# The up projection of a feed-forward block: the norm's root applied to the finished tiles in PSUM instead of to its input

## The reference

```python
y = memory_cross_attention(h, ...)          # ends in o @ wo, MEM_INNER 512 -> 2048
x = x + rmsnorm(y, g[3])
h = rmsnorm(x, g[4])
y = conv_ffn(h, ffn_w_up, ffn_conv_w, ffn_conv_b, ffn_w_down)

def rmsnorm(x, gain):
    return x * rsqrt(mean(x * x, axis=-1) + 1e-6) * gain

def conv_ffn(h, w_up, conv_w, conv_b, w_down):
    up = h @ w_up                           # [256, 11264]
    up_pad = pad(up, 2 tokens in front)
    conv = conv_b + sum(up_pad[:, j:j + s] * conv_w[j] for j in range(3))
    gate, val = split(conv, 2)
    return (gelu(gate) * val) @ w_down
```

## Time and profile before

| what | us |
|---|---|
| median of 3 runs (3180.01 to 3181.32) | 3180.11 |
| the profiled execution | 3179.2 |
| its span | 3177.4 |
| TensorE busy | 3040.5 |
| VectorE busy | 1570.8 |
| ScalarE busy | 1266.5 |

### The profile page before, as it was taken

One profiled execution on the slowest core, in us unless ns is written; L12 is line 12 of the kernel. 1 busy time (PEld: TensorE's weight loads), 2 busy tenths in 40 slices (PEclk: granted clock), 3 DMA queues, 4 the chain that ended last, 5 costly groups with the idle time before them and its releaser, 6 DMA issues.

```text
span 3177.4 us, 51930 instructions
## 1 busy us (share of the span) xinstructions
PE 3040.5 (96%) x21496; PEld 2642.4 (83%) x21496; DVE 1570.8 (49%) x2402; ACT 1266.5 (40%) x1925; POOL 17.9 (1%) x34
## 2 busy tenths in 40 slices
PE   6999999899889999999998999999999999999997
PEld 6966666698779999999996888778878998889896
DVE  4444434544365556564445323554553474247744
ACT  4322112343445444443434223444542472245544
POOL 0000000000000000000000000000000000000000
PEclk9999999899989999999999999999999999999998
DMA  7577777544435555545553222222223443234442
GB/s 231 183 292 313 311 316 286 199 141 151 146 119 183 179 181 184 182 156 181 175 191 110 93 93 80 80 80 90 91 99 119 159 161 105 92 118 146 141 152 106
DMA packets 74279, 509.69 MB, mean 160 GB/s; under 512 B 8460, under 2 KB 8588, under 8 KB 20240
## 3 DMA queue, kind: packets, MB, share of 16 engines
q1 hardware_dynamic: 70416, 486.08, 42.9%
q0 software_dynamic: 3712, 21.40, 2.1%
HBM read 500.89 MB, written 6.55 MB: 160 GB/s over the span
## 4 chain that ended last, share of the span: by engine, by line
PE 87%; DVE 6%; ACT 3%; DMA 2%; issue 1%; SPq 0%; ACTq 0%; DVEq 0%
PE bank L685 39%; PE bank L1220 8%; PE bank L780 5%; PE bank L1251 5%; PE bank L1253 5%; PE bank L1252 5%; PE bank L797 2%; PE bank L730 1%; PE bank L731 1%; PE bank L732 1%; PE bank L936 1%; PE bank L876 1%; DMA high_f<-in_w_in 1%; DVE ring_f32r L1972 1%; PE bank L1289 1%
## 5 line engine op out<-in xcount | busy, mean ns | idle before, releaser
L1972 DVE TENSOR_TENSOR ring_f32r<-ring_f,high_f32r 128x1024 fp32r<-128x1024 f32 (+1 forms) x692 | 780.7, 1159 | 794.8 <-ACT high_f32r L1405 793.5
L1405 ACT CAST high_f32r<-ring_f 128x1024 fp32r<-128x1024 f32 (+1 forms) x692 | 655.8, 997 | 881.4 <-PE bank L685 535.9
L685 PE MATMUL bank<-y_f32r,high_f32r 128*128 128x256 f32 (+1 forms) x2784 | 852.6, 306 | 23.3 <-DVE ring_f32r L1972 10.9
L685 PE MATMUL bank<-h_f32r,high_f32r 128*128 128x256 f32 (+1 forms) x2208 | 685.9, 311 | 4.3 <-DVE y_f32r L1972 3.4
L685 PE MATMUL bank<-y_f32r,ring_f32r 128*128 128x256 f32 (+1 forms) x2208 | 673.3, 305 | 0.0
L685 PEld LDWEIGHTS bank<-y_f32r,high_f32r 128*128 128x128 f32 x2784 | 535.3, 192 | 47.1 <-issue 22.2
L685 PEld LDWEIGHTS bank<-h_f32r,high_f32r 128*128 128x128 f32 x2208 | 422.9, 192 | 26.7 <-issue 4.5
L685 PEld LDWEIGHTS bank<-y_f32r,ring_f32r 128*128 128x128 f32 x2208 | 424.2, 192 | 17.2
L1251 PE MATMUL bank<-h_f32r,high_f32r 128*128 128x512 f32 x512 | 209.3, 409 | 0.0
L780 PE MATMUL bank<-h_f,high_f 128*128 128x256 f32 x768 | 196.4, 394 | 9.5 <-DMA high_f<-in_w_in 9.5
L1253 PE MATMUL bank<-h_f32r,ring_f32r 128*128 128x512 f32 x512 | 200.1, 391 | 0.0
(11 more groups left out here) (413 smaller groups left out, 4925.1 us busy)
## 6 DMA issues: line engine op xcount, KB each, us to landing
ring_f<-in_w_in SPq DMA_DIRECT2D x135, 1024.0 KB, 4.9
ring_f<-in_w_mod SPq DMA_DIRECT2D x96, 1024.0 KB, 8.9
ring_f<-in_w_up SPq DMA_DIRECT2D x88, 1024.0 KB, 4.9
ring_f<-in_w_out SPq DMA_DIRECT2D x56, 1024.0 KB, 4.9
ring_f<-in_w_down SPq DMA_DIRECT2D x64, 704.0 KB, 4.0
high_f<-in_w_in SPq DMA_DIRECT2D x24, 1024.0 KB, 5.0
ring_f<-in_w_kv SPq DMA_DIRECT2D x8, 1024.0 KB, 5.0
ring_f<-in_w_q SPq DMA_DIRECT2D x4, 1024.0 KB, 4.9
```

The lines of the kernel that those rows point to most:

```text
L685: last = mm(bk[(t0 + j) % banks][:, 0:width], w[:, c], x[:, k], start=(k == 0 and w is hi and x is rhs.hi), stop=(k == KC - 1 and w is lo))
L1405: act.copy(w_hi[p % 2][:, half], slot[s % SLOTS][:, half]).then_inc(w_high, 1)
L1972: return v.tensor_tensor(out, in0, in1, op)
```

## The change

- ACT's copy of each `wo` tile to Z takes the gain of the first norm with it as a scale column.
- DVE multiplies Z by the root alone, in pieces of 1024 columns, and adds it to x; between the quarters it makes the low halves of H.
- H is now x times the gain of the second norm, without the root. ACT makes it, four instructions of 256 columns per quarter, and casts the quarter right behind it.
- ACT squares x afterwards, into 16 free tiles of Z. PE sums these squares between up tiles 1 and 2, and the second root is made from there.
- DVE multiplies every finished up tile by the root, in its bank, before ACT reads it. ACT waits for that (`f_scaled`) instead of for the tile.

```diff
+        up_sq = Z[:, 16:32]
...
             finish_sum(T, 7)
-            colsum4(H[0], T, 7)
-            gemm3("up")
+            gemm3("up", 0, 2)
+            colsum4(up_sq, T, 7)
+            gemm3("up", 2, 86, rhs="up")
...
                 b = bk[(TILE0["wo"] + n) % 2][:, 0:T]
-                act.copy(Z[:, n, :], b)
+                f(Z[:, n, :], b, ACT.Identity, scale=vec("g")[:, 3 * KC + n:3 * KC + n + 1])
...
             root()
-            squares_of_x(2)
+            for q in range(4):
+                act.wait_ge(x_ready, 4 + q + 1)
+                for k in range(4 * q, 4 * q + 4):
+                    last = f(H[0][:, k, :], X[0][:, k, :], ACT.Identity, scale=vec("g")[:, 4 * KC + k:4 * KC + k + 1])
+                last.then_inc(rhs_made, 1)
+                rhs_highs("up", (q,))
+            for q in range(4):
+                f(up_sq[:, 4 * q:4 * q + 4], X[0][:, 4 * q:4 * q + 4], ACT.Square).then_inc(sq_ready, 1)
             root()
-
-            rhs_highs("up")
...
-                act.wait_ge(gemm_done, i * 4 + (TILE0["up"] + j + 1))
+                act.wait_ge(S("f_scaled"), i * 4 + (j + 1))
...
             rstd(D, RMS1_EPS, parts=True)
             for q in range(4):
-                add_quarter(Z[:, 0:16], gains(3), q)
+                c = slice(4 * q, 4 * q + 4)
+                step(tt(Z[:, c], Z[:, c], spread(stat[:, 0:T], 4)))
+                tt(X[0][:, c], X[0][:, c], Z[:, c], ALU.add).then_inc(x_ready, 1)
+                if q:
+                    rhs_low("up", q - 1)
+            rhs_low("up", 3)
             rstd(D, RMS1_EPS, parts=True)
-            rhs_made_and_split("up", norm_quarter(H[0], X[0], gains(4)))
...
             def up(j, i, ahead=("up", 2)):
+                par, b, c = at(convf, i * 4 + j), bk[(TILE0["up"] + j) % 4], cv[j % 4]
+                dve.wait_ge(gemm_done, i * 4 + (TILE0["up"] + j + 1))
+                tt(b[:, 0:T], b[:, 0:T], stat[:, 0:T]).then_inc(S("f_scaled"), 1)
                 dve.wait_ge(S("f_part"), i * 4 + (j + 1))
-                par, b, c = at(convf, i * 4 + j), bk[(TILE0["up"] + j) % 4], cv[j % 4]
```

## The result

| | before | changed |
|---|---|---|
| median of 20 runs, us | 3179.41 | 3186.76 |
| lowest to highest | 3176.32 to 3183.39 | 3183.87 to 3191.16 |
| the profiled execution | 3179.2 | 3191.16 |
| its span | 3177.4 | 3189.2 |

The changed kernel takes 1.0023 times as long, with an interval of 1.0017 to 1.0028: 7.4 us more, by the interval 5.4 to 8.9. The forecast of 3185.4 is 1.4 us under the median, and its range held it. The kernel is slower clear of the noise; the 6.4 us that I called no change lie inside the interval, so on which side of them it falls is not settled. The difference itself was forecast at 5.3 us, just under the interval.

What follows compares the result with a forecast made beforehand. PE, busy 3040.5 of 3177.4 us, was taken as the bound. Terms -2.0 + 1.6 + 2.1 + 1.9 + 1.7 = +5.3 us on 3179.2 give 3184.5, plus 0.9 for the median: 3185.4 us, range 3180.5 to 3190.

Steps and rivals of the forecast that it cites:

- steps 1 to 7: Chain from the first norm through tiles 0, 1 and the sum: tile 2 starts at 905.95, 2.0 us earlier.
- step 3: ACT makes H, casts it, DVE subtracts: PE starts tile 0 at 877.45, 16 us earlier than now.
- step 8: Half clock returns in tile 2 after the hole, the first one hidden by tile 0's quarters: 1.6 us lost.
- step 5: Sum of squares behind tile 1: PE's small matmuls take 2.4 us, end at 897.0, and the root is there at 901.1.
- The mark: Start of tile 2 in the kernel before, taken as about 907.98, against which the new start was compared.
- half of either is lost: Half clock after the hole, held 2.7 or 3.8 us: a loss of 1.35 to 1.9 us, taken as 1.6.
- The loop: Up tiles: 88 scalings of 0.42 us, 37 us of DVE work, leave 0.95 us of room, so 86 tiles cost nothing.
- The second rival: Scaling in the bank dearer than a read: at 1.6 us each the kernel takes 3203 us; chance 0.05.
- The two places behind DVE's splits: After tiles 62 and 86 ACT waits for a scaling behind DVE's split: PE's waits grow by 2.1 and 1.9 us.
- I count one fall: +1.7: PE's clock falls behind only one of the two late waits of about 3.0 and 2.9 us, costing 1.7 us.
- shifts with it and grows no further: PE's 2.69 us wait, following the one after tile 86's split, moves later without getting longer.
- The first rival: Clock falls in both late stalls behind DVE's splits: 1.7 us more, +7.0 in all, 3187.1 us; chance 0.33.

Runs made afterwards that it cites:

- e3: Changed kernel with the scalings of tiles 63 and 87 put between the halves of DVE's split of finished tiles: 3183.29 us, 1.0013 of before.
- e2: Changed kernel without the scaling in the bank (second root made, not applied), so the new front alone: 3178.91 us, 0.9998 of before.
- e10: Second run of the changed kernel without the scaling in the bank: 3178.39 us, 0.9998 of before.
- e1: Kernel before with only the scaling of each up tile in its bank added (root applied twice): 3184.08 us, 1.0012 of before.
- e9: Second run of the kernel before with only the scaling in the bank added: 3183.33 us, 1.0011 of before.
- the fastest version: Changed kernel, sum between tiles 0 and 1, tile 2's weights before tile 0's scaling, late scalings between split halves: 3171.80 us (0.9980), again 3172.31 (0.9981).
- e5: Changed kernel with the weight halves of tiles 2 and 3 made ahead of the second root: 3177.77 us, 0.9999 of before.
- e6: Changed kernel, weights of tiles 2 and 3 ahead of the second root, late scalings between DVE's split halves: 3173.74 us, 0.9985 of before.

## Why the prediction was right, and where not

**The path to tile 2 (steps 1 to 7): right in kind, 1.2 us off.** Seen from the norm's sum, tile 2 starts after 41.26 us, where the steps give 40.03 (865.92 to 905.95). Tile 0's first matmul at 880.85 is the 877.45 of step 3 moved by 3.4, and the last low half at 889.49 is its 886.1; up to there the steps hold. Tile 0's last quarter then ran mostly at half clock (until 892.7), which step 8 had as hidden, and the sum ended about 0.5 us later than in step 5. ACT's root came as expected, but DVE's reciprocal began 0.95 us after its last instruction for 0.60 before, with ACT's 0.42 in between. Between the end of the reciprocal and the scaling, and between the scaling and ACT, lie 0.3 and 0.27 us where I had put 0.05 in all: the chain shows DVE's sequencer at L2379 there, the entry of the loop over the tiles. Before, that entry lay beside tile 0.

The mark was misread as well. 907.98 is about when tile 1 is handed to ACT; tile 2's first matmul is at 907.59, and 905.95 was compared with the wrong one. Both together turn the forecast of 2.0 us earlier into 0.4.

**Step 8: right that the half clock comes back, too small.** I took 1.6 us. It lasted 5.9 us of work, and from tile 2's start to the first late wait's end it is 4.75 us more than before, of which the wait is 2.09: the half clock cost 2.66. In the five traces with this hole it lasted 2.9, 3.3, 5.8, 5.9 and 6.2 us. The step's "half of either is lost" is a little too much: at half clock 26 matmuls were busy in 5.60 us, at full clock 47 in 5.70 (e3), so 0.44 of the time is lost. Its 2.7 and 3.8 us were the lengths of the stretches asked for; the clock came back after 2.9 and 4.1. The front, forecast at 0.4 us faster, was 2.25 slower in this execution (2.66 less 0.41), and level by the ratios of e2 and e10, where the half clock was short.

**The loop: right.** 88 scalings at 432 ns are 38 us of DVE and move no ordinary tile. The second rival had nothing: the room was 0.95 us and the excess over a read 0.01.

**The two places behind DVE's splits: right to 0.1 us.** Forecast +2.1 and +1.9; the waits grew from 0.89 to 2.98 and from 1.01 to 2.82. e1 and e9 show them without the new front, e2 and e10 the front without them, and e3 that the order of two instructions makes 2.3 us of it.

**The clock behind them is the step that failed: "I count one fall: +1.7".** In this execution it fell behind both. The first fall lasted for 5.9 us of work: from the first late wait's end to the second's it is 142.07 us for 137.69, 4.38 more, of which the second wait's growth is 1.81 and the fall 2.57. The second fall lasted 3.4 us and cost nothing, since the third wait ends 6.9 us behind the second whatever the clock does in between, and shrank from 2.69 to 1.20. That give-back was in none of my steps; I had written that this wait "shifts with it and grows no further", which was true and missed that it can shrink. In all five traces with a fall behind the second wait, the way from that wait's end to the second model is the 268.18 us of before, to 0.01.

The sum by measured distances is -0.41 + 2.66 + 2.09 + 1.81 + 2.57 + 0 = 8.72, and the trace has 8.7. Against the 5.3 forecast the front's path gave 1.6 less, step 8 cost 1.1 more and the late clock 0.9 more, all to the same side. That the forecast time is still only 1.4 us off is partly luck: the 3 runs that I started from had a median 0.7 above that of the 20, and the medians differ by 7.4, less than the 8.7 of the profiled executions.

The first rival, both falls and 3187.1, named what happened in this execution, and of the cases it came nearest to the median. But its price was wrong: it gave the second fall 1.7 us, which was worth nothing, and took the first for 1.7 where it cost 2.6. The Trainium skill's page "TensorE: Matmul & The Clock Gate", in its section "HAM oscillation — how this bites in real kernels", warns of long idle gaps between bursts of matmuls; that its rule covers waits as short as these was my reading of it. In the traces the clock fell behind nine of the twelve waits of 2.81 to 2.98 us, as the next section but one counts.

**What stays open.** By the medians the two halves cost about +4 and about -1 us, 3 together, and the whole costs 7.4 and 8.3. The intervals of the parts are some 3 us to either side each, so a part of the gap can be noise. The stretches in the traces say 5.7 and 3.9 for the scaling, 2.1 and 1.2 for the front, 8.7 and 9.1 for both, some 2.5 us more than the parts. In the traces this gap is the clock's: the half clock behind the hole lasted 5.8 to 6.2 us in the three traces with the scaling and 2.9 and 3.3 in the two without, and the fall behind the first late wait about 6 us in both of the whole, 3.4 or none in e1 and e9. Why it lasts longer in the whole, and whether it does so in the executions without a trace, is not shown.

## What to carry to other kernels

When work is moved off a chain's head, follow it to where it lands: here 16 us won ahead of the first tile came down to 0.4 us at the third, because the sum, the root and the next weights' preparation lost the tile that had covered them. An instruction added in front of an engine that used to run alone costs nothing where the other engine is free, and costs the other engine's longest block where it is not: put it into the middle of that block. The mends together, in the fastest version, turned 0.2% lost into 0.2% won. And a loss just ahead of a wait that another engine ends costs nothing, up to the length of that wait.

## What the runs showed of the hardware

The same wait of PE does not always bring the clock down. Counted over the thirteen traces at the three late places, each wait reached at full clock: behind 2.96 to 2.98 us the clock fell in four of six cases, behind 2.81 to 2.82 in five of six, behind 2.69 to 2.71 in two of eight, and behind those of 0.89 to 1.81, eighteen in all, never. The two traces with a wait of 2.00 us inside the sum (e5, e6) show a fall of 3.4 us at the start of tile 2; whether the sum's narrow matmuls have a part in it is not shown.

Of the eleven falls at the late places, three began 0.7 us or more before PE started again and lasted for 5.9 to 6.1 us of work; eight began within 0.1 us of its start or up to 1.6 us behind it and lasted 3.3 to 3.4. Where nothing took the loss in, a fall of 3.4 us cost 1.5 us (e1 and e5 at the first place, e2 and e6 at the third), and one of 5.9 or 6.0 cost 2.6. So two executions of one kernel with the same first two waits to 0.01 us differed by 1.8 us in that stretch (e1 and e9), and a sum of terms cannot say more of it than a chance.

A product of DVE in place in a bank cost 432 ns for 128x256 fp32, 11 more than one that only reads a bank and writes elsewhere.
